# Neighbourhood attention with the probabilities turned by a product with the diagonal of 1/sum, and outputs that leave turned

## The reference

```python
def block(args):
    ...
    s_loc = jnp.einsum("bqhd,bnhd->bhqn", qi, kb).astype(jnp.float32) * scale + bias.astype(jnp.float32)
    s_loc = jnp.where(mask, s_loc, NEG_INF)
    s_ctx = jnp.einsum("bqhd,bnhd->bhqn", qi, kc).astype(jnp.float32) * scale
    p = jax.nn.softmax(jnp.concatenate([s_loc, s_ctx], axis=-1), axis=-1).astype(vb.dtype)
    n_loc = nbr * GRID_W
    return (jnp.einsum("bhqn,bnhd->bqhd", p[..., :n_loc], vb)
            + jnp.einsum("bhqn,bnhd->bqhd", p[..., n_loc:], vc))
o = lax.map(block, (jnp.arange(nblk), q_blocks))
y_lat = o.swapaxes(0, 1).reshape(bsz, n_lat, NA_WIDTH) @ w_out
```

## Time and profile before

| what | value |
|---|---|
| median of 3 runs | 3601.56 us (3596.17 to 3604.36) |
| the profiled execution's own time | 3592.47 us |
| its span in the trace | 3590.6 us |
| TensorE busy | 2805.2 us, 78% |
| VectorE busy | 1229.1 us, 34% |
| ScalarE busy | 806.8 us, 22% |
| mean granted TensorE clock | 0.877 of full |

### The profile page before, as it was taken

One profiled execution on the slowest core, in us unless ns is written; L12 is line 12 of the kernel. 1 busy time (PEld: TensorE's weight loads), 2 busy tenths in 40 slices (PEclk: granted clock), 3 DMA queues, 4 the chain that ended last, 5 costly groups with the idle time before them and its releaser, 6 DMA issues. The chain is left out here.

```text
span 3590.6 us, 44146 instructions
## 1 busy us (share of the span) xinstructions
PE 2805.2 (78%) x17820; PEld 1902.8 (53%) x17820; DVE 1229.1 (34%) x1842; ACT 806.8 (22%) x1126; POOL 245.1 (7%) x214
## 2 busy tenths in 40 slices
PE   5667589999990497387788726998368989989799
PEld 4546334444440474332222216985346979887598
DVE  2344411111116424400000044427734445444353
ACT  1141011111110212111111104411223434333343
POOL 0001410000004000200000020000000000000000
PEclk8888799999995699689989867999688999996699
DMA  5454569999988411689999954423043434341342
GB/s 236 200 232 174 218 258 419 423 422 422 422 349 298 130 66 55 225 361 427 428 428 427 400 175 192 184 94 120 3 176 117 187 141 187 141 150 48 141 179 96
DMA packets 125189, 839.02 MB, mean 234 GB/s; under 512 B 33528, under 2 KB 35640, under 8 KB 70872
## 3 DMA queue, kind: packets, MB, share of 16 engines
q1 hardware_dynamic: 87832, 742.16, 51.3%
q0 software_dynamic: 20544, 50.39, 3.8%
q10 hardware_dynamic: 16640, 44.05, 3.2%
HBM read 792.39 MB, written 63.14 MB: 238 GB/s over the span
## 5 line engine op out<-in xcount | busy, mean ns | idle before, releaser
L1344 PE MATMUL psum<-experts_ahead_ring_up,moe_cols 128*64 128x512 f32 x2048 | 455.4, 597 | 0.0
L1888 PE MATMUL psum<-second_x_hi,ffn_up_hi 128*128 128x256 f32 x1408 | 402.8, 286 | 45.5 <-DVE ffn_up_lo L1963 45.5
L1888 PE MATMUL psum<-second_x_lo,ffn_up_hi 128*128 128x256 f32 x1408 | 402.1, 286 | 0.0
L1888 PE MATMUL psum<-second_x_hi,ffn_up_lo 128*128 128x256 f32 x1408 | 402.0, 285 | 0.0
L1365 PE MATMUL psum<-experts_ahead_ring_down,experts_ahead_counting 128*64 128x512 f32 x1024 | 273.9, 683 | 104.2 <-issue 104.2
L1888 PEld LDWEIGHTS psum<-second_x_hi,ffn_up_hi 128*128 128x128 f32 x1408 | 274.2, 195 | 48.5 <-DVE ffn_up_lo L1963 47.1
L1344 PEld LDWEIGHTS psum<-experts_ahead_ring_up,moe_cols 128*64 128x64 f32 x2048 | 141.9, 137 | 267.5 <-issue 265.5
L1888 PEld LDWEIGHTS psum<-second_x_lo,ffn_up_hi 128*128 128x128 f32 x1408 | 274.2, 195 | 1.4
L1888 PEld LDWEIGHTS psum<-second_x_hi,ffn_up_lo 128*128 128x128 f32 x1408 | 274.0, 195 | 0.0
L1555 DVE TENSOR_TENSOR experts_gated<-experts_silu,psum 128x256 f32<-128x256 f32 (+1 forms) x104 | 38.5, 370 | 616.0 <-ACT experts_silu L1469 616.0
L1963 DVE TENSOR_TENSOR ffn_up_lo<-second_ring_up,ffn_up_hi 128x4096 fp32r<-128x4096 f32 x44 | 194.4, 4425 | 121.3 <-ACT ffn_up_hi L1925 121.3
(11 more groups left out here) (424 smaller groups left out, 4343.0 us busy)
## 6 DMA issues: line engine op xcount, KB each, us to landing
experts_ahead_ring_up<-in_experts SPq DMA_DIRECT2D x138, 2048.0 KB
experts_ahead_ring_down<-in_experts SPq DMA_DIRECT2D x138, 1024.0 KB, 16.9
second_ring_up<-in_ffn SPq DMA_DIRECT2D x44, 2048.0 KB
second_ring_down<-in_ffn SPq DMA_DIRECT2D x44, 1024.0 KB, 4.9
results<-experts_y ACTq DMA_DIRECT2D x64, 512.0 KB
second_ring_up<-in_attn_w_qkv SPq DMA_DIRECT2D x9, 2048.0 KB, 7.7
results<-ab_att_zeros SPq DMA_DIRECT2D x28, 512.0 KB, 13.6
ab_ahead_ab_in_w<-in_w_mod SPq DMA_DIRECT2D x6, 2048.0 KB
```

The costliest lines, as they stand in the source:

```text
L1344: last = nc.tensor.matmul(psum[64 * e:64 * e + 64, bank, :], x[:, k, 64 * e:64 * e + 64], w[:, k, :, :].rearrange("p a n -> p (a n)"), sta ...
L1888: last = nc.tensor.matmul(psum[:, 2 * m + kind, 0:LAT], w[:, j, k, at], h[:, k, :], start=k == 0 and which == 0, stop=k == KD - 1 and whic ...
```

## The change

The attention stage gets a flag `turned_outs`, which only na_att sets. With it, VectorE takes the reciprocal of a row's sum before the turning and writes the diagonal matrix `inverse` (identity times 1/sum, 128x128). TensorE turns the probabilities by a product with this matrix in place of a transpose, so that they come out turned and already divided. The value product then has the values stationary and the turned probabilities moving, and its result has the head's channels on the partitions, which is what "na_out" needs. The output scaling becomes a plain copy into a new buffer `outs`, and the stage "na_o" is gone. TensorE now waits for `inverse_ready` where it waited for `probs_ready`.

```diff
@@ attention_stage, TensorE, step - 1
-                    pe.wait_ge(probs_ready, u + 1)
+                    pe.wait_ge(inverse_ready if turned_outs else probs_ready, u + 1)
...
-                        last = nc.tensor.transpose(turned_ps[:, c * P:(c + 1) * P], probs[:, u % 2, c * P:(c + 1) * P], ident[:])
+                        if turned_outs:
+                            last = nc.tensor.matmul(turned_ps[:, c * P:(c + 1) * P], probs[:, u % 2, c * P:(c + 1) * P], inverse[:, u % 2, :], start=True, stop=True)
...
@@ attention_stage, TensorE, step - 2
+                        if turned_outs:
+                            last = nc.tensor.matmul(psum[0:dh, 6 + u % 2, 0:P], v, probs_t[:, u % 2, c * P:(c + 1) * P],
+                                                    start=c == 0, stop=c == len(vs) - 1)
@@ attention_stage, VectorE, behind the bias instructions of the step
                         chain.then(ins)
+                if turned_outs and 0 <= step - 1 < n:
+                    u = step - 1
+                    dve.wait_ge(probs_ready, u + 1)
+                    chain.then(nc.vector.reciprocal(inv_total[:, u:u + 1], total[:, u:u + 1]))
+                    nc.vector.tensor_scalar(inverse[:, u % 2, :], ident[:], inv_total[:, u:u + 1], None, ALU.mult).then_inc(inverse_ready, 1)
+                if step < n:
+                    u = step
                     chain.then(nc.vector.reduce_max(peak[:, u:u + 1], exp_source(u), X_AXIS))
...
                     dve.wait_ge(outs_ready, u + 1)
+                    if turned_outs:
+                        nc.vector.tensor_copy(out(units[u]), psum[0:dh, 6 + u % 2, 0:P]).then_inc(outs_used, 1)
+                        continue
@@ first_block
+                outs = st.sbuf("outs", [P, NA_HEADS, LAT])
...
-                    lambda u: acc[:, u[1], u[0] * HEAD:(u[0] + 1) * HEAD], HEAD)
-
-                transpose_stage(nc, "na_o", psum, ident, NA_HEADS, 2, lambda j, t: acc[:, t, j * HEAD:(j + 1) * HEAD],
-                                lambda engine, j, bank: copy_on(nc, engine, q[:, j, :], bank[:, 0:LAT]))
-                rows_product(nc, "na_out", psum, q, out_stream, KD, 2, to_rows(acc))
+                    lambda u: outs[:, u[0], u[1] * P:(u[1] + 1) * P], HEAD, turned_outs=True)
+                rows_product(nc, "na_out", psum, outs, out_stream, KD, 2, to_rows(acc))
```

More of the change, by code:

```diff
@@ L649, in modulated_cols, with attention_stage @@
                           lambda j: cols[0][:, j, :], lambda j: cols[1][:, j, :], affine)
-def attention_stage(nc, name, psum, ident, units, score_parts, n_keys, bias, scale, values, out, dh, idle_fill=None):
+def attention_stage(nc, name, psum, ident, units, score_parts, n_keys, bias, scale, values, out, dh, idle_fill=None, turned_outs=False):
     n = len(units)
@@ L673, in attention_stage @@
         chain_sem = st.sem("chain")
+        if turned_outs:
+            inverse, inverse_ready = st.sbuf("inverse", [P, 2, P]), st.sem("inverse_ready")
         block = st.block()
@@ L720, in _ @@
                     for c in range(n_keys(units[u]) // P):
-                        last = nc.tensor.transpose(turned_ps[:, c * P:(c + 1) * P], probs[:, u % 2, c * P:(c + 1) * P], ident[:])
+                        if turned_outs:
+                            last = nc.tensor.matmul(turned_ps[:, c * P:(c + 1) * P], probs[:, u % 2, c * P:(c + 1) * P], inverse[:, u % 2, :], start=True, stop=True)
+                        else:
+                            last = nc.tensor.transpose(turned_ps[:, c * P:(c + 1) * P], probs[:, u % 2, c * P:(c + 1) * P], ident[:])
                     last.then_inc(turned, 1)
@@ L730, in _ @@
                     for c, v in enumerate(vs):
-                        last = nc.tensor.matmul(psum[:, 6 + u % 2, 0:dh], probs_t[:, u % 2, c * P:(c + 1) * P], v,
-                                                start=c == 0, stop=c == len(vs) - 1)
+                        if turned_outs:
+                            last = nc.tensor.matmul(psum[0:dh, 6 + u % 2, 0:P], v, probs_t[:, u % 2, c * P:(c + 1) * P],
+                                                    start=c == 0, stop=c == len(vs) - 1)
+                        else:
+                            last = nc.tensor.matmul(psum[:, 6 + u % 2, 0:dh], probs_t[:, u % 2, c * P:(c + 1) * P], v,
+                                                    start=c == 0, stop=c == len(vs) - 1)
                     last.then_inc(outs_ready, 1)
```

## The result

| | kernel before | changed kernel |
|---|---|---|
| median | 3595.62 us (10 runs) | 3615.86 us (10 runs) |
| profiled execution, span | 3590.6 us | 3609.9 us |
| first weights of na_att to first weights of na_out | 53.90 us | 72.96 us |
| distance from scores to scores in na_att | 2.78 us | 4.28 us |

The changed kernel is slower: the ratio is 1.0053, with a 95% interval from 1.0037 to 1.007. That is 0.53%, or 19 us of 3595.62, and by the interval 13 to 25 us; 19.9 us were forecast. The median of the kernel before was 3601.56 us over 3 runs and is 3595.62 us over 10, and the changed kernel's lies about as far, 5.6 us, under the 3621.5 us forecast; the ratio is what counts.

The account below looks back on a forecast made before the run. No engine was taken as full: a loop of waits through two units bounds the stage. 2.97 + 18.48 (middle) + 1.51 - 3.07 = +19.9 us on the profiled 3592.47; from the median 3601.56, 3621.5 us, range 3609 to 3635.

Parts of the forecast that it names:

- The new loop: In na_att, scores, bias, reciprocal, diagonal, turning and values form a loop through one unit: 4.32 us per unit against 2.78.
- The start: First steps of na_att, begun at half clock: the third scores after the start come 2.97 us later.
- The end: From the scores of unit 15 to the last output copied in na_att: 8.87 us against 7.36, +1.51 us.
- What goes: The stage na_o with its barrier disappears ahead of na_out: -3.07 us.
- The sum: Whole kernel: start, middle, end and the removed stage add up to +19.9 us, all reaching the end.
- The product costs four times the transpose: Rival on the turning in na_att: 0.67 us more per unit, 3632 us; chance 0.05.
- The clock stays at half: Rival on TensorE's clock in na_att: half clock adds 2.77 us a unit, 3662 us; chance 0.05.
- The old loop still binds: Rival in na_att: the period stays at 2.78 us and only na_o's 3.07 us go, 3598.5 us; chance 0.05.
- The argument from the Fourier stages: Against half clock in na_att: Fourier stages keep 1.00 with TensorE busy 2.66 and 1.51 of 4 us; here 2.64 of 4.32.
- TensorE becomes the bound in part: Rival in na_att: waits overlap more than counted, period near 3.2 us, +3 us, 3605 us; chance 0.03.

Follow-up runs that it names:

- product alone: Changed kernel, turning by a product with the identity, waiting only for the exponential, reciprocal and diagonal left out: 3588.19 us, one execution, against 3598.88 for the kernel before.
- wait alone: Changed kernel with the turning again a transpose, still waiting for the diagonal: 3605.77 us, one execution, against 3598.88 for the kernel before.
- Diagonal last: Changed kernel with reciprocal and diagonal moved behind the negative maximum of the next unit: 3653.72 us, one execution, against 3598.88 for the kernel before.

## Why the prediction was right

The mechanism was right: the diagonal stands behind a bias that waits for the scores, which closes a loop through one unit. The experiments move its length as this loop says. The sum was 19.9 us, and its terms stand as follows.

- **The new loop.** Forecast 4.32, measured 4.28 us. Five of its seven pieces (1.17, 0.79, 0.20, 0.89, 0.89) came to the hundredth, and the diagonal takes the 0.29 us that were taken for it; the hand-over is 0.05 us instead of 0.09. Over 12 units 18.00 us came for the 18.48 forecast.
- **The start.** 2.82 us for 2.97. The clock rose some 9 us after the first scores, early enough that the turning of unit 1 already ran at full speed, as assumed. That this came within 0.2 us of the profile before is luck: the moment lies between 4.5 and 9.2 us in the eleven profiles, and the profile with the earliest has a stage 2 us shorter than one of the same code.
- **The end.** 1.29 us for 1.51. Of the 0.22 us less, some 0.1 is the hand-over again, which comes twice. The rest is that the last reciprocal follows the copy of an output after 0.21 us (1414.72 and 1414.93), where 0.32 was taken.
- **What goes.** 3.05 us for 3.07: 0.75 us from the last output to na_out, 3.80 before.
- **The sum.** 2.82 + 18.00 + 1.29 - 3.05 = 19.06 us, which is the growth of the stage. That it reaches the whole time is borne out by the ratio within its interval, 13 to 25 us.

Of the rivals:

- *The product costs four times the transpose*: it loads in 0.97 us, x8, and the next work starts 0.89 us behind it, like V. The price was 0.50 us, which "product alone" and "wait alone" confirm from two sides. The Trainium skill's factor of 4 for the FP32 transpose mode ("TensorE: Matmul & The Clock Gate", Terms) is not seen here: in this kernel it is 0.89 against 0.39 us of TensorE's time, a factor of 2.3.
- *The clock stays at half*: it did not, but it was closer than its chance said. The change leaves TensorE waiting 1.37 us a unit for the diagonal at a clock of 1.00. "Diagonal last" leaves 2.15 us, and its clock is 0.76. The argument from the Fourier stages held for the change; it was a busy share over a few microseconds, and the gap that recurs was not in it.
- *The old loop still binds*: refuted by the order of the waits. Even where it does bind ("product alone", 3.03 us), the distance is above the 2.97 us that the text gave as the point below which the change is no loss, and the stage is 0.89 us longer.
- *TensorE becomes the bound in part*: no. The score loads are 4.28 us apart, and TensorE's own work is 2.64.

What the prediction did not see is how the two costs combine. Taking the 3.05 us of na_o out, the wait alone adds 64.50 + 3.05 - 53.90 = 13.65 us, the product alone 3.94, and both together 22.11, which is 4.5 more than their sum. The product's 0.50 us counts whole in a loop through one unit and half in a loop through two, which is 3.0 us of it over 12 units; the other 1.5 us come in the first steps and the last, where the clock's rise plays in.

## What to carry to other kernels

In a hand-pipelined loop, ask of each new operand not how long it takes but which instruction it stands behind, and whether that one waits for the engine that will wait for the operand. Here 0.5 us of VectorE's work closed a loop TensorE - VectorE - TensorE through one unit and cost 1.0 us a unit, and moving it ahead of the bias took that back: 3.04 us with the product, against 3.03 where nothing waits for a diagonal. Then price what replaces a cheap form (16 x 4 fp32 transposes by products) against what it saves (one stage of 3.05 us): even without any wait the products gave back what the stage had cost (3.94 us for 3.05, in one profile each).

## What the runs showed of the hardware

TensorE's clock can fall in work that waits for a short time in every unit. With 1.37 us of waiting in each 4.28 us (the changed kernel) the granted clock was 1.00 from 1356 to 1410. With 2.15 us in each step of some 5.1 us at full clock ("diagonal last") it moved between 1.2 and 2.4 GHz inside the steps and came to 0.76 on the mean, which in the step shown made the products behind the gap nearly twice as long, 3.36 for 1.78 us, and so lengthened the loop from about 5.1 to 6.54 us. Here the wait on the path cost more than its own length. Whether it was the length of the gap or the smaller share of work in a step is not separated by these runs.

VectorE started the next instruction 0.20 us after the diagonal's start, though the diagonal itself is recorded with 0.29 us (1382.33 to 1382.53): with no chained wait between them they overlap. The reciprocal ahead of it, with a chained wait behind it, is recorded with 0.16 us and the diagonal starts 0.20 us after it. So the recorded duration lay above what an instruction added to its engine in one case and below it in the other, and the distance from start to start is the price.
